# Before the first product of x in a five-mixer network: loads, value products, norm blocks and squares reordered

## The chip, the cores and the metric

The program runs on one core of a Trainium2 chip. Its engines are PE (matrix products), ACT (one-input functions), DVE and POOL (two-input arithmetic), and SP, which here only issues transfers between HBM and the on-chip memory. The metric is the device time of one execution in microseconds (us). What is changed lies wholly in the first part of the program, up to the point where the first product of `x` starts, apart from one rule for norms that holds in later places too.

## The reference, cut to what matters

The reference runs an attention block of two layers on `x` (1024 tokens of width 1024) with a memory `mem` (256 rows of width 1024), and then a pooling mixer and a convolutional feed-forward block. This is what the change touches:

```
memn = rmsnorm(mem, mem_norm_gain)                     # 256 x 1024
for l in range(2):
    h = rmsnorm(x, norm_gain[l])                       # 1024 x 1024
    mk, mv = split(memn @ w_mem_kv[l], 2, axis=-1)     # 256 x 512 each, 4 heads of 128
    qa, ka, ... , qm, gate = split_cols(h @ w_in[l], ...)
    ...
    ym = softmax(qm @ mk.T * 128 ** -0.5) @ mv         # for each of the 4 heads
    ...
# rmsnorm(x, g) = x * rsqrt(mean(x * x) + 1e-6) * g
```

All of it is float32. The kernel keeps that precision by writing each operand as a high part and a low part in the matmul's own format and adding three products (high by high, high by low, low by high).

## The kernel before, in words

**Layout.** `x` and `mem` lie transposed: 128 of the 1024 features to a partition block `c` (eight blocks), tokens along the free dimension. `x` is handled as two halves of 512 tokens; `mem` is one piece of 256 rows. The weights come as units of 256 KB (128 partitions by 512 numbers) from HBM into a ring of three slots, tile `WR`. Each unit is cut into two sub-units of 256 columns. For each sub-unit ACT writes the high part into `WS` (a ring of six), and POOL or DVE subtracts it from the original to give the low part (L2235 on POOL, L1895 on DVE). PE then multiplies (L1420 to L1422, three products for each block of features).

**Order.** A list `steps` is filled once by ordinary Python, and each engine's program walks it from front to back, doing its own share of each step and waiting on semaphores. So the order on every engine, and in SP's queue of transfers, is the order in which `put(...)` was called. `pump()` advances the weight products by one sub-unit (and lets deferred work go on by a step); `ahead(i)` puts the split of a sub-unit five before its product, and the load of a unit `NRAW` = 3 before its use. The norms are generators that `yield` between their parts, and the loop `for _ in first_norm()` calls `pump()` once for each `yield`, which is how norm work and products of the memory are interleaved.

**The start.** SP issues `mem`, four small constants, the eight blocks of `x` (tile `X`), and then the weights. The norm of `mem` comes first: eight squares on ACT, added up on DVE (L2060), a sum over partitions on PE (L1586), the root on POOL (L2224), a broadcast on PE (L1600), and then the eight blocks in `norm_split`: scale on DVE (L2096), high part on ACT, low part on DVE or POOL by turns (L2103, L2256). Only then come the first weight splits. ACT starts by waiting for the four constants.

**The memory's products.** 16 projections, for each layer four heads of keys (`mk`) and four heads of values (`mv`), use 32 units, that is 64 sub-units of six 128x256 products. All have the weights as the stationary operand and the memory as the moving one, so the result lies features by rows. For the values that is the wrong way round: ACT copies the result to `F1`, PE turns it in two 128x128 transposes (L1468), and ACT and DVE take the high and low part from there.

**The norm of x**, during these products: 16 squares (block 0 of both halves, block 1 of both halves, ...), then root, broadcast and eight blocks of the first half, then the same for the second half. After 40 `yield`s it is done, the products of the memory that are left follow, and then the first product of `x` (`HT` by `WS`) starts.

Of the kernel before, what the change touches and what calls it, by code (L numbers as in the profile page):

```python
# [15 lines left out]
MEM = 256  # L16
# [10 lines left out]
NRAW, NSPL = 3, 6  # L27
B_S, B_PT, B_O, B_X = 2, 4, 6, 7
# [130 lines left out]
def build(nc, d):  # L159
    ctx = ExitStack()  # L160
    with ctx:
# [33 lines left out]

        GQ = EO[:, 3072:3200].rearrange("p (a f) -> p a f", a=2)
# [69 lines left out]
        d_const, d_mem = signal("d_const"), signal("d_mem")  # L266
        d_x = [signal(f"d_x{c}") for c in range(8)]
        d_raw = [signal(f"d_raw{i}") for i in range(NRAW)]
# [38 lines left out]

        def ahead(i):
            while at["split"] < min(i + NSPL - 1, len(subs)):
                no = at["split"]  # L310
                u = subs[no][0]
                while at["load"] <= min(u + NRAW - 1, len(units) - 1):
                    v = at["load"]
                    put("load", v)
                    raw_at.append(d_raw[v % NRAW].add(16 * len(units[v](v % NRAW))))
                    at["load"] += 1
                s_whi.add()
                on = s_wlov if no < at["both"] and no % 3 else s_wlop
                half_lo.append((on, on.add()))
                put("split", no)  # L320
                at["split"] += 1

        def w_cols(src, k0, kn, cols):
            n = sum(c[1] for c in cols)

            def pieces(slot):
                v = WR[:, slot, 0:kn * n].rearrange("p (k n) -> p k n", n=n)
# [8 lines left out]
        def w_rows(src, tiles, c0):  # L336
            kn, width = len(tiles), src.shape[1]

            def pieces(slot):
                o, out = 0, []  # L340
                for i, (row, m) in enumerate(tiles[0]):
                    step = tiles[1][i][0] - row
                    out.append((WR[o:o + m, slot, 0:128 * kn].rearrange("p (k n) -> p k n", n=128),
# [19 lines left out]
        OPS = {"hl": (1, 1), "q": (2, 2), "k": (4, 4), "kg": (4, 4), "qg": (2, 2), "v": (1, 0), "vg": (3, 0), "rope": (1, 0), "gate": (1, 1), "x": (0, 1)}  # L363
# [8 lines left out]
        def leave(h):  # L372
# [24 lines left out]
            if h.kind in ("hl", "q", "qg"):  # L397
                ready[h.to[0]] = [(s_ed, s_ed.n)]
# [684 lines left out]
        d_mem.add(16)  # L1083
        for c in range(8):
            square(mem_norm, c, (d_mem, 16))
        for _ in close(mem_norm):
            pass
        for _ in norm_split(mem_norm, C_MEMG, mem_at, MRING, [], [(d_mem, 16)] * 8):
            pass
        for layer in (0, 1):  # L1090
# [14 lines left out]
        def first_norm():  # L1105
            yield
            yield
            for c in range(8):
                for n in (0, 1):
                    square(x_norm[n], c, xt[c])  # L1110
                    yield
            for n in (0, 1):
                yield from close(x_norm[n])
                yield
                yield from norm_split(x_norm[n], C_G0, ht_half(n), HRING, [(s_nd, 8)] if n == 0 else x_norm[0].lo[4:], xt)
# [218 lines left out]
        at["both"] = len(subs)  # L1334
# [4 lines left out]
        for _ in first_norm():  # L1339
            if at["task"] < mem_tasks:  # L1340
                pump()
# [58 lines left out]

        def v_parts(h, i):
# [5 lines left out]
            if h.width == 256:  # L1407
                v = v_at(slot).rearrange("p (h t x c) -> p h t x c", h=4, t=2, x=2)[:, h.to[3]]
# [1046 lines left out]
```

## Time and profile before

| | before |
|---|---|
| median of 3 runs | 2588.92 us (2580.43 to 2593.25) |
| the profiled execution | 2589.86 us, its span 2588.1 us |
| mean granted PE clock | 0.979 of full |
| PE busy (share of the span) | 2424.2 us (94%) |
| DVE busy | 1328.4 us (51%) |
| ACT busy | 1214.3 us (47%) |
| POOL busy | 854.7 us (33%) |
| transfers | 191.93 MB, mean 74 GB/s |

The span is what the trace covers of the profiled execution, and 1.8 us lie around it. Over the whole span PE is nearly always busy; its busy share in the first of 40 slices (64.7 us each) is five tenths and in the second eight tenths, while nearly all others are eight or nine tenths. Times of instructions overlap in the pipelines (the start of the next one, not the end of the last, gives the pace).

### The profile page before, as it was taken

How to read it: one execution, taken by the hardware profiler on the slowest of the kernel's cores; microseconds unless marked ns; L12 is line 12 of the kernel's file. 1: busy time of each engine (PE TensorE's matmuls, PEld its weight loads, DVE VectorE, ACT ScalarE, POOL GpSimd, SP SyncE). 2: the span in 40 equal slices, each digit the busy share in tenths (PEclk: the TensorE clock that was granted, in tenths of full speed). 3: DMA queues.
4: the chain of work that ended last, by engine and by line, in shares of the span. 5: the costliest groups of instructions: out<-in, count | busy, mean ns of one | idle time of the engine just before them, and what ended most of it. 6: DMA issues, size and time to landing. Idle time of an engine off the chain costs nothing.

```text
span 2588.1 us, 36197 instructions
## 1 busy us (share of the span) xinstructions
PE 2424.2 (94%) x12584; PEld 2038.8 (79%) x12584; DVE 1328.4 (51%) x2748; ACT 1214.3 (47%) x2884; POOL 854.7 (33%) x1053
## 2 busy tenths in 40 slices
PE   5898889999999999999999999998889999999999
PEld 5787777777887878888888888776667888888877
DVE  5443576776787524345555555677775313312331
ACT  4443455665676434445556556554454313322321
POOL 2332211111125553221222222556675422322322
PEclk8898999999999999999999999999999999999999
DMA  4421210111124242222222223522223211111112
GB/s 155 131 70 46 57 29 17 33 33 35 44 66 147 78 127 90 89 71 78 86 86 79 78 86 104 165 74 73 66 81 91 74 49 45 49 46 52 49 49 86
DMA packets 309924, 191.93 MB, mean 74 GB/s; under 512 B 63728, under 2 KB 288240, under 8 KB 309232
## 3 DMA queue, kind: packets, MB, share of 16 engines
q1 hardware_dynamic: 309744, 189.61, 25.0%
q8 instruction: 103, 1.69, 0.3%
q14 instruction: 77, 0.63, 0.1%
HBM read 170.16 MB, written 19.40 MB: 73 GB/s over the span
## 4 chain that ended last, share of the span: by engine, by line
PE 75%; DVE 9%; ACT 5%; issue 5%; POOL 3%; DMA 2%; SPq 0%; DVEq 0%; ACTq 0%; POOLq 0%
PE PS L1420 20%; PE PS L1422 19%; PE PS L1421 19%; PE PS L1559 4%; PE PS L1526 4%; PE PS L1513 2%; POOL WS L2235 2%; PE PS L1514 2%; PE PS L1570 2%; ACT PY L1648 1%; DVE ST L1986 1%; ACT PT L1648 1%; DVE PY L2060 1%; ACT WS L1648 1%; ACT EO L1648 1%
## 5 line engine op out<-in xcount | busy, mean ns | idle before, releaser
L2235 POOL TENSOR_TENSOR WS<-WR,WS 128x256 fp32r<-128x256 f32 (+1 forms) x946 | 731.7, 792 | 1609.7 <-ACT WS L1648 1608.6
L1420 PE MATMUL PS<-HT,WS 128*128 128x512 f32 x2080 | 838.3, 403 | 44.2 <-POOL WS L2235 22.4
L1422 PE MATMUL PS<-HT,WS 128*128 128x512 f32 x2080 | 816.0, 392 | 0.0
L1421 PE MATMUL PS<-HT,WS 128*128 128x512 f32 x2080 | 815.2, 392 | 0.0
L1648 ACT ACTIVATE WS<-WR 128x256 fp32r<-128x256 f32 x988 | 368.3, 408 | 384.5 <-PE PS L1422 343.6
L1420 PEld LDWEIGHTS PS<-HT,WS 128*128 128x128 f32 x2080 | 394.0, 189 | 143.4 <-issue 34.4
L1422 PEld LDWEIGHTS PS<-HT,WS 128*128 128x128 f32 x2080 | 393.2, 189 | 84.8
L1421 PEld LDWEIGHTS PS<-HT,WS 128*128 128x128 f32 x2080 | 394.4, 190 | 74.3
L1648 ACT ACTIVATE PT<-PS 128x512 fp32r<-128x512 f32 x352 | 186.3, 530 | 244.0 <-PE PS L1526 243.6
L1864 DVE TENSOR_TENSOR PT<-PS,PT 128x512 fp32r<-128x512 f32 x352 | 208.4, 608 | 93.8 <-ACT PT L1648 92.6
L1420 PE MATMUL PS<-QKV,WS 128*128 128x512 f32 (+1 forms) x608 | 232.7, 383 | 21.8 <-POOL WS L2235 11.2
L1421 PE MATMUL PS<-QKV,WS 128*128 128x512 f32 (+1 forms) x608 | 228.9, 376 | 0.0
L1422 PE MATMUL PS<-QKV,WS 128*128 128x512 f32 (+1 forms) x608 | 228.5, 376 | 0.0
L1559 PE MATMUL PS<-PT,QKV 128*128 128x256 f32 (+1 forms) x1248 | 211.4, 291 | 12.2 <-DVE YB L2050 11.3
L1559 PEld LDWEIGHTS PS<-PT,QKV 128*128 128x128 f32 x1248 | 180.6, 193 | 24.6 <-issue 18.1
L1648 ACT ACTIVATE QKV<-PS 64x512 fp32r<-64x512 f32 (+2 forms) x212 | 122.3, 577 | 157.2 <-PE PS L1422 128.1
L1526 PE MATMUL PS<-ID,PY 128*128 128x128 f32 x1072 | 186.5, 278 | 0.0
L1420 PEld LDWEIGHTS PS<-QKV,WS 128*128 128x128 f32 x608 | 120.3, 198 | 45.7 <-ACT WS L1648 20.7
L1513 PE MATMUL PS<-QKV 128*128 128x384 f32 (+2 forms) x320 | 123.0, 386 | 23.4 <-ACT PY L1648 13.6
L1865 DVE SCALAR_TENSOR_TENSOR QKV<-PS,QKV 64x512 fp32r<-64x512 f32 (+1 forms) x112 | 77.2, 689 | 128.1 <-ACT QKV L1648 125.7
L1648 ACT ACTIVATE PY<-PY,ST 128x384 f32<-128x384 f32 (+1 forms) x192 | 115.5, 601 | 48.2 <-DVE ST L2006 38.2
L1421 PEld LDWEIGHTS PS<-QKV,WS 128*128 128x128 f32 x608 | 120.6, 198 | 18.8
(160 smaller groups left out, 2739.8 us busy)
## 6 DMA issues: line engine op xcount, KB each, us to landing
WR<-in_ffn_in SPq DMA_DIRECT2D x120, 256.0 KB, 2.9
WR<-in_w_in_odd SPq DMA_DIRECT2D x106, 256.0 KB, 3.0
EO<-in_grid SPq DMA_DIRECT2D x48, 384.0 KB, 3.1
WR<-in_w_in_even SPq DMA_DIRECT2D x100, 128.0 KB, 2.6
WR<-in_w_out_odd SPq DMA_DIRECT2D x48, 256.0 KB, 2.9
yd<-PY SPq DMA_DIRECT2D x44, 256.0 KB, 3.4
WR<-in_w_in_even SPq DMA_DIRECT2D x34, 256.0 KB, 3.0
WR<-in_w_mem SPq DMA_DIRECT2D x32, 256.0 KB, 2.9
```

What stands on the lines that cost most here:

```text
L1420: e.matmul(out, wh, rh, start=start, stop=False)
L1421: e.matmul(out, wh, rl, start=False, stop=False)
L1422: return e.matmul(out, wl, rh, start=False, stop=stop)
L1513: e.matmul(out, q, kh, start=True, stop=False)
L1514: m = e.matmul(out, q, kl, start=False, stop=True)
L1526: m = e.transpose(PS[:, B_PT + pb, o + 128 * z:o + 128 * z + 128], p_at(job.c, job.scores[x].slot, p0, p0 + 128), ID[:, :])
L1559: m = e.matmul(out, vv, p, start=a, stop=b)
L1570: m = e.matmul(PS[n * h:n * h + n, B_X, 128 * x:128 * x + 128], RD[:, f.pp % 2, x, h:h + 1].to_broadcast([128, n]), ID[:, :], start=True, ...
L1648: return e.activation(out, in_, func, **more)
L1864: return e.tensor_tensor(out, src, f32(hi), ALU.subtract)
L1865: return e.scalar_tensor_tensor(out=out, in0=src, scalar=scale, in1=f32(hi), op0=ALU.mult, op1=ALU.subtract)
L2235: e.tensor_tensor(WS[:, i % NSPL, 1, 0:n], WR[:, u % NRAW, o:o + n], f32(WS[:, i % NSPL, 0, 0:n]), ALU.subtract).then_inc(s_wlop.sem, 1)
```

## The change

Six things are changed, all in the order of the steps or the place of data:

- The weights of the memory use seven slots (`RAW`: the three of `WR` and four pieces of tiles that are idle then), and six units are loaded ahead of `x`. The later weights keep three slots.
- `mem` is loaded in two halves, ACT no longer waits for the constants at its start (each weight split does), and a one-column square on ACT comes ahead of everything.
- The first five weight splits stand behind the sum of the memory's norm and ahead of its root and blocks.
- The memory's values are produced with the memory as the stationary operand and two heads' weights as the moving one (`mv`, step kind `memT`): 2 projections a layer with 8 sub-units each. The copy to `F1` and the transposes are gone; ACT and DVE take high and low part of 512 columns at once.
- In `norm_split` the scaling of block `c` is put a step ahead of its high part. This holds for every norm that uses it: memory, `x`, the second layer's and the feed-forward's.
- The squares go by halves: eight of the first half, then the first half's root and blocks interleaved with the squares of the second half. There are 42 `yield`s now, with one and two `pump()`s by turns. Low parts of the memory's weights go to POOL and DVE by turns (before: one in three to POOL).

```
+MEM_UNITS, MEM_RAW = 32, 7
+        RAW = [WR[:, i, :] for i in range(NRAW)] + [PY[:, 1024:1536], PY[:, 1536:2048], F1[:, :], SG[:, 0:512]]
+        def raw_slot(u):
+            return u % MEM_RAW if u < MEM_UNITS else (u - MEM_UNITS) % NRAW
         def ahead(i):
             while at["split"] < min(i + NSPL - 1, len(subs)):
                 no = at["split"]
                 u = subs[no][0]
-                while at["load"] <= min(u + NRAW - 1, len(units) - 1):
...
+                while at["load"] <= min(u + (MEM_RAW if at["load"] < MEM_UNITS else NRAW) - 1, len(units) - 1):
+                    load_next()
                 s_whi.add()
-                on = s_wlov if no < at["both"] and no % 3 else s_wlop
+                on = s_wlov if no < at["both"] and no % (2 if no < 2 * MEM_UNITS else 3) else s_wlop
...
         def norm_split(nm, col, dst, ring, before, need):
-            for c in range(8):
-                nm.nd[c], nm.nh[c] = s_nd.add(), s_nh.add()
-                on = s_nlv if c % 2 else s_nlp
-                nm.lo[c] = (on, on.add())
-                put("nsplit", nm, c, need[c])
+            for c in range(9):
+                if c < 8:
+                    nm.nd[c] = s_nd.add()
+                    put("nscale", nm, c, need[c])
                 if c:
-                    put("nsplit lo", nm, c - 1)
-                yield
-            put("nsplit lo", nm, 7)
+                    nm.nh[c - 1] = s_nh.add()
+                    put("nsplit", nm, c - 1)
+                if c > 1:
+                    low_part(nm, c - 2)
+                if c:
+                    yield
+            low_part(nm, 7)
...
-            for h in range(4):
-                c0 = [(512 + 128 * h, 128)]
-                proj(f"mv{layer}{h}", [w_cols(w, 0, 4, c0), w_cols(w, 4, 4, c0)], "v", (f"mv{layer}", None, layer, h), ("mem", 0), MEM)
+            for g in range(2):
+                c0 = [(512 + 256 * g, 256)]
+                proj(f"mv{layer}{g}", [w_cols(w, k, 2, c0) for k in (0, 2, 4, 6)], "mv", (f"mv{layer}", None, layer, g), ("memT", 0), 512)
+        for c in range(8):
+            square(mem_norm, c, (d_mem[c // 4], 16))
+        for _ in range(6):
+            load_next()
+        put("x load")
+        closing = close(mem_norm)
+        next(closing)
+        ahead(0)
...
             for c in range(8):
-                for n in (0, 1):
-                    square(x_norm[n], c, xt[c])
-                    yield
-            for n in (0, 1):
-                yield from close(x_norm[n])
+                square(x_norm[0], c, xt[c])
+                yield
+            split = first_half()
+            for c in range(8):
+                next(split)
+                yield
+                square(x_norm[1], c, xt[c])
+                yield
+            flush_acc()
+            for _ in split:
+                yield
+            yield from close(x_norm[1])
...
-        for _ in first_norm():
-            if at["task"] < mem_tasks:
-                pump()
+        for i, _ in enumerate(first_norm()):
+            for _ in range(1 + i % 2):
+                if at["task"] < mem_tasks:
+                    pump()
...
+                        if h.rhs[0] == "memT":
+                            for x in (0, 1):
+                                m = three(PS[:, h.bank, 256 * x:256 * x + 256], mh[:, 128 * x:128 * x + 128], ml[:, 128 * x:128 * x + 128],
+                                          wh, wl, j == 0 and x == 0, end and x == 1)
...
-            w.wait_ge(d_const, 64)
+            w.wait_ge(s_init, 1)
+            act(YB[:, 0:1], ON[:, :], ACT.Square)
```

SP, the start of its queue, before (`WR` are weight slots, `X` is x):

```order
L2287 DMA EO<-in_memT 128x8x256
L2288 DMA COL<-in_cols 128x240
L2289 DMA ID<-in_ident 128x128
L2290 DMA PCT<-in_pct 128x64
L2291 DMA SK<-in_sink 128x8
L2293 DMA X<-in_xT 128x1024 x8
L2304 DMA WR<-in_w_mem 128x4x128 x32
```

SP at the same place with the change (`PY`, `F` and `SG` hold four more weight slots):

```order
L2349 DMA EO<-in_memT 128x4x256 x2
L2350 DMA COL<-in_cols 128x240
L2351 DMA ID<-in_ident 128x128
L2352 DMA PCT<-in_pct 128x64
L2353 DMA SK<-in_sink 128x8
L2369 DMA WR<-in_w_mem 128x4x128 x3
L2369 DMA PY<-in_w_mem 128x4x128 x2
L2369 DMA F<-in_w_mem 128x4x128
L2357 DMA X<-in_xT 128x1024 x8
L2369 DMA SG<-in_w_mem 128x4x128
```

Six weight units moved ahead of the eight loads of x; the seventh follows them.

ACT, its first instructions, before (`PY<-EO` are the memory's squares, `QKV<-EO` its high parts, `WS` the weights' high parts, `PY<-X` squares of x):

```order
L1648 ACT_TABLE_LOAD
L1648 ACTIVATE PY<-EO 128x256 x8
L1648 ACTIVATE QKV<-EO 128x256 x8
L1648 ACTIVATE WS<-WR 128x256 x6
L1648 ACTIVATE PY<-X 128x512
L1648 ACTIVATE WS<-WR 128x256
```

ACT at the same place with the change:

```order
L1699 ACT_TABLE_LOAD
L1699 ACTIVATE YB<-ON 128x1
L1699 ACTIVATE PY<-EO 128x256 x8
L1699 ACTIVATE WS<-WR 128x256 x5
L1699 ACTIVATE QKV<-EO 128x256 x8
L1699 ACTIVATE WS<-WR 128x256
L1699 ACTIVATE WS<-PY 128x256
L1699 ACTIVATE PY<-X 128x512
```

Five weight splits moved from behind the memory's high parts to ahead of them.

DVE, the start of the first half's blocks of x, before (`SS` the mean, `EO<-X` a scaled block, `HT` a low part of x, `WS` a low part of weights, `QKV<-PS` a result):

```order
L2067 TENSOR_SCALAR SS<-PS 128x4
L1895 TENSOR_TENSOR WS<-WR,WS 128x256 x2
L1864 TENSOR_TENSOR QKV<-PS,QKV 128x2x128
L2096 SCALAR_TENSOR_TENSOR EO<-X,COL,PS 128x512
L1895 TENSOR_TENSOR WS<-WR,WS 128x256
L2096 SCALAR_TENSOR_TENSOR EO<-X,COL,PS 128x512
L1895 TENSOR_TENSOR WS<-WR,WS 128x256
L2096 SCALAR_TENSOR_TENSOR EO<-X,COL,PS 128x512
L2103 TENSOR_TENSOR HT<-EO,HT 128x512
```

DVE at the start of these blocks with the change (`PY<-PY` adds up squares, now those of the second half):

```order
L1951 TENSOR_TENSOR WS<-WR,WS 128x256
L2156 SCALAR_TENSOR_TENSOR EO<-X,COL,PS 128x512 x2
L2120 TENSOR_TENSOR PY<-PY 128x512
L1951 TENSOR_TENSOR WS<-PY,WS 128x256
L1920 TENSOR_TENSOR QKV<-PS,QKV 128x4x128
L2156 SCALAR_TENSOR_TENSOR EO<-X,COL,PS 128x512
L1951 TENSOR_TENSOR WS<-PY,WS 128x256
L2120 TENSOR_TENSOR PY<-PY 128x512
L1951 TENSOR_TENSOR WS<-F,WS 128x256
```

Two blocks are scaled before the first one is split, and additions of the second half's squares stand between. From the first product of x on, PE's instructions are the same in the same order; in DVE's four later norm halves one scaling each stands earlier.

## Rows read from the trace of the kernel before

**Rows 1.** The page's head.

```profile
span 2588.1 us, 36197 instructions
```

**Rows 2.** Waits of PE between 22 and 113.7 us: total, times, longest.

```profile
PE PS L1586 <- DVE PY L2060: 3.4, 1, 3.4
PE PS L1586 <- DVE QKV L1864: 2.3, 1, 2.3
```

**Rows 3.** Stretches: length, busy (count) by engine, PEclk, DMA share, GB/s.

```profile
22.00:42.40 20.40, 16.07 (x108) 15.03 (x108) 16.94 (x32) 15.98 (x41) 6.22 (x7) 1.00 0.44 129
42.40:50.00 7.60, 7.57 (x38) 7.57 (x39) 1.42 (x4) 0.92 (x3) 1.86 (x2) 0.55 0.24 71
50.00:68.60 18.60, 9.00 (x52) 8.37 (x51) 13.29 (x21) 9.45 (x23) 6.85 (x6) 0.77 0.20 56
93.00:113.70 20.70, 19.03 (x138) 18.38 (x138) 9.31 (x21) 10.76 (x32) 7.75 (x12) 0.89 0.54 154
```

**Rows 4.** The timeline at the start: start us, length us, engine, line, operation.

```profile
6.28 1.28 ACT L1648 ACT_TABLE_LOAD   x1 [6.28 <-DMA EO<-in_memT]
8.33 3.61 DVE L2060 TENSOR_TENSOR PY<-PY 128x256 f32<-128x256 f32 x7 [7.43 <-ACT PY L1648]
13.37 0.71 POOL L2224 TENSOR_TENSOR SM<-SM,MH 128x2 f32<-128x2 f32 x1 [12.93 <-DVE SM L2067]
15.39 1.26 DVE L2096 SCALAR_TENSOR_TENSOR EO<-EO,COL,PS 128x256 f32<-128x256 f32 x3 [2.17 <-PE PS L1600]
22.06 0.55 PE L1420 MATMUL PS<-QKV,WS 128*128 128x256 f32 x1 [6.71 <-POOL WS L2235]
```

**Rows 5.** Stretches at the start, columns as in rows 3.

```profile
0.00:6.00 6.00, 0.00 (x0) 0.00 (x0) 0.09 (x2) 0.00 (x0) 0.20 (x4) 1.00 0.69 208
6.00:12.00 6.00, 0.00 (x0) 0.00 (x0) 2.98 (x7) 4.17 (x9) 0.00 (x0) 1.00 0.98 349
```

**Rows 6.** The timeline of PE: a pair each at two paces.

```profile
26.05 0.28 PE L1421 MATMUL PS<-QKV,WS 128*128 128x256 f32 x1
26.17 0.28 PE L1422 MATMUL PS<-QKV,WS 128*128 128x256 f32 x1
...
44.36 0.41 PE L1422 MATMUL PS<-QKV,WS 128*128 128x256 f32 x1
44.58 0.41 PE L1420 MATMUL PS<-QKV,WS 128*128 128x256 f32 x1
```

**Rows 7.** The timeline of DVE and POOL where both work.

```profile
85.81 1.27 POOL L2256 TENSOR_TENSOR HT<-EO,HT 128x512 fp32r<-128x512 f32 x1 [1.32 <-ACT HT L1648]
...
86.07 1.28 DVE L1895 TENSOR_TENSOR WS<-WR,WS 128x256 fp32r<-128x256 f32 x1 [0.40 <-ACT WS L1648]
...
107.49 0.74 POOL L2235 TENSOR_TENSOR WS<-WR,WS 128x256 fp32r<-128x256 f32 x1 [2.92 <-ACT WS L1648]
...
107.72 0.42 DVE L1864 TENSOR_TENSOR QKV<-PS,QKV 128x256 fp32r<-128x256 f32 x1 [2.53 <-ACT QKV L1648]
```

**Rows 8.** The timeline of DVE, back to back.

```profile
30.19 0.41 DVE L1895 TENSOR_TENSOR WS<-WR,WS 128x256 fp32r<-128x256 f32 x1
30.53 0.68 DVE L2060 TENSOR_TENSOR PY<-PY 128x512 f32<-128x512 f32 x1
31.13 0.41 DVE L1895 TENSOR_TENSOR WS<-WR,WS 128x256 fp32r<-128x256 f32 x1
```

**Rows 9.** The first product of x, and the stretch behind it.

```profile
113.44 0.48 PE L1420 MATMUL PS<-HT,WS 128*128 128x512 f32 x1
...
113.40:200.00 86.60, 86.60 (x451) 74.28 (x451) 29.51 (x70) 33.88 (x94) 32.45 (x43) 1.00 0.33 102
```

**Rows 10.** Groups of PE between 22 and 113.7 us: count, busy, mean ns.

```profile
L1586 PE MATMUL PS<-ON,PY 128*128 128x1 f32 x16 | 3.3, 330 | 5.7 <-DVE PY L2060 3.4 <-DVE QKV L1864 2.3
L1600 PE MATMUL PS<-ID,SS 128*128 128x128 f32 x16 | 3.2, 370 | 0.0
```

**Rows 11.** Waits of PE between 960 and 985 us.

```profile
PE PS L1420 <- POOL HT L2256: 2.5, 2, 1.5
```

More of the change, by code:

```diff
@@ L264, in bias_at @@
             return EO[:, o:o + 768].rearrange("p (h n) -> p h n", h=2)
-        d_const, d_mem = signal("d_const"), signal("d_mem")
+        d_const, d_mem = signal("d_const"), [signal(f"d_mem{i}") for i in range(2)]
         d_x = [signal(f"d_x{c}") for c in range(8)]
-        d_raw = [signal(f"d_raw{i}") for i in range(NRAW)]
+        d_raw = [signal(f"d_raw{i}") for i in range(MEM_RAW)]
         d_y = [signal(f"d_y{i}") for i in range(2)]
@@ L306, in add_units, with load_next @@
             return first, tiles
+        def raw_slot(u):
+            return u % MEM_RAW if u < MEM_UNITS else (u - MEM_UNITS) % NRAW
+        def load_next():
+            v = at["load"]
+            put("load", v)
+            raw_at.append(d_raw[raw_slot(v)].add(16 * len(units[v](raw_slot(v)))))
+            at["load"] += 1
         def ahead(i):
@@ L1082, in build @@
         mem_norm = Norm(lambda c: MX[:, c, :], MEM, SM, 0, B_O)
[L1083 to L1089, printed above, removed]
         for layer in (0, 1):
@@ L1094, in build @@
                 proj(f"mk{layer}{h}", [w_cols(w, 0, 4, c0), w_cols(w, 4, 4, c0)], "hl", (f"mk{layer}", None, layer, 1.0, h), ("mem", 0), MEM)
-            for h in range(4):
-                c0 = [(512 + 128 * h, 128)]
-                proj(f"mv{layer}{h}", [w_cols(w, 0, 4, c0), w_cols(w, 4, 4, c0)], "v", (f"mv{layer}", None, layer, h), ("mem", 0), MEM)
+            for g in range(2):
+                c0 = [(512 + 256 * g, 256)]
+                proj(f"mv{layer}{g}", [w_cols(w, k, 2, c0) for k in (0, 2, 4, 6)], "mv", (f"mv{layer}", None, layer, g), ("memT", 0), 512)
+        assert len(units) == MEM_UNITS
+        at["both"] = len(subs)
+        for i in range(2):
+            d_mem[i].add(16)
+        for c in range(8):
[6 more added lines that the diff above has]
+        ahead(0)
+        for _ in closing:
+            pass
+        for _ in norm_split(mem_norm, C_MEMG, mem_at, MRING, [], [(d_mem[1], 16)] * 8):
+            pass
         x_norm = [Norm(half_of(n), 512, SS, 512 * n, B_S + n) for n in (0, 1)]
@@ L1694, in scalar_program @@
                     slot = h.to[2]
-                    if h.kind == "hl" and h.rhs[0] == "mem":
+                    if h.kind == "mv":
+                        src, hi, _ = mem_v_parts(h)
+                        act(hi, src).then_inc(s_ea.sem, 1)
+                    elif h.kind == "hl" and h.rhs[0] == "mem":
                         m0 = 256 * h.to[4]
@@ L2286, in sync_program @@
             w = Waits(e)
-            e.dma_start(MX, d["memT"].rearrange("(c p) n -> p c n", p=128)).then_inc(d_mem.sem, 16)
+            slot_unit = {}
+            for i in range(2):
+                e.dma_start(MX[:, 4 * i:4 * i + 4, :], d["memT"][512 * i:512 * i + 512, :].rearrange("(c p) n -> p c n", p=128)).then_inc(d_mem[i].sem, 16)
             e.dma_start(COL[:, :], d["cols"]).then_inc(d_const.sem, 16)
@@ L2291, in sync_program @@
             e.dma_start(SK[:, :], bass.AP(d["sink"].tensor, 0, [[0, 128], [1, 8]])).then_inc(d_const.sem, 16)
[L2292 to L2293 removed]
             for kind, *of in steps:
[L2295 removed]
+                if kind == "x load":
+                    for c in range(8):
+                        e.dma_start(X[:, c, :], d["xT"][128 * c:128 * c + 128, :]).then_inc(d_x[c].sem, 16)
+                elif kind == "load":
                     u, = of
[L2297 to L2301 removed]
+                    slot = raw_slot(u)
+                    if slot in slot_unit:
+                        v = slot_unit[slot]
+                        w.wait_ge(s_whi, unit_last[v] + 1)
+                        for sig, value in raw_done[v]:
                             w.wait_ge(sig, value)
+                    slot_unit[slot] = u
                     for dst, src in units[u](slot):
```

63 lines of the change are left out of this document (34 added, 29 removed).

## The prediction

> **What bounds the kernel now.** I read the page first for the span [rows 1], then cut the time up to the first product of x into stretches [rows 3], then the timeline by engine. The reader should see a start in two parts. Until 22.06 us PE has no weight product at all [rows 4]. From there to 113.44 us, where the first product of x starts [rows 9], PE has 64 sub-units of six products and little else. At the fast pace two products start 0.12 us apart (26.05, 26.17), so a sub-unit is 0.72 us and all of them 46.1 us; the part takes 91.4 us. It is lost in two ways. PE waits, since the norm of x takes DVE and ACT: 9.00 us of 18.60 busy between 50.0 and 68.6 [rows 3]. And behind idle stretches the granted clock falls from 1.00 (2.4 GHz) to its lower level (1.2 GHz): 0.55, 0.77 and 0.89 on the mean in three stretches [rows 3], where two products start 0.22 us apart (44.36, 44.58) [rows 6]. Behind 113.4 us PE is busy for 86.60 of 86.60 us at clock 1.00 [rows 9]. PE's instructions from there on are the same before and after, and no step there stands at a fixed time, so what the start gains, the end gains: the forecast is the move of that 113.44 us.
>
> **The start, step by step.** Table load: it runs from 6.28 to 7.56 us, behind the landing of `mem` [rows 4]; now a one-column square brings it forward under the transfer: -1.3 us. Halves of `mem`: the DVE's seven additions take 3.61 us and end at 11.94, a pace of 0.53 us [rows 4]. With the first half there early (an estimate: at 4.5 us of the 6.2 that the whole takes) only four additions stand behind the second landing: 6.2, a square of about 0.4, and 4 x 0.53 make 8.9, 3.0 us sooner with the table load in it. If the halves land together only the 1.3 is left. The sum, root and broadcast stay: DVE's first scaling is 3.45 us behind the last addition (15.39 against 11.94), now at 12.4. POOL's root ends 2.14 us behind it (14.08), now at 11.1.
>
> Next the weights: five high parts go ahead on ACT, three low parts on POOL and two on DVE. POOL's low part is 0.74 us [rows 7], so three take POOL to 13.3, one more for the memory's first block to 14.1. The first product is at 14.2 instead of 22.06. The last weights that this needs (units 0 to 2, 0.79 MB, behind 1.05 MB of `mem` and 0.23 MB of constants) are 2.07 MB; 208 GB/s for 6 us bring 1.25 MB, the rest comes at 349 GB/s [rows 5]: 8.3 us. On ACT the eight high parts of the memory are queued behind these splits, and DVE, POOL and PE wait for them; there are 4 us of cover till 12.4. Without the cover each us late is a us lost. Bounds for the first product: 13.4 (low parts ahead of the root) and 17.5 (halves together, and weights late by 1 to 2 us).
>
> x now has six units ahead of it: its first block is complete at 3.37 MB, 12.1 us, and all of it 3.67 MB later at about 349 GB/s, near 22.6 us [rows 5]. Its squares start behind the seventh split, some 18 us, and need a block each 1.6 us or so. ACT would stand with all weight splits behind it if x were late; I cost it at nothing, hidden by the memory's first key products.
>
> **The middle.** What limits 64 sub-units and the norm of x together? One row decides it. A low part on DVE is 0.41 us long (30.19) [rows 8], but the one at 86.07 takes 1.28 and ends at 87.35, 0.27 behind the end (87.08) of POOL's 1.27 us low part of x [rows 7]. DVE instructions with two on-chip-memory inputs and POOL's take turns. The one at 107.72, which has one input in PSUM, keeps its 0.42 under POOL's 0.74 [rows 7]. So there is a shared lane, and its load behind 14.2 us is, with durations where undisturbed and starts back to back [rows 7, 8]:
>
> POOL: 29 low parts of the memory's weights and 4 of the first of x's, 33 x 0.74 = 24.4; 8 low parts of x, 8 x 1.27 = 10.2; 4 of the memory, 3.0. Sum 37.6.
> DVE: 30 low parts at 0.34 (30.19 to 30.53) = 10.2; 14 additions at 0.60 (30.53 to 31.13) = 8.4; 8 low parts of x at the same 0.60 = 4.8; 4 of the memory at 0.34 = 1.4. Sum 24.8.
>
> Together 62.4 us. The scalings (one input in PSUM) and the results stay off the lane. POOL's larger share costs: 11 low parts moved from 0.34 to 0.74 are 4.4 us of it. PE needs 46.1 plus 6.5 for sums and broadcasts [rows 10], ACT less than either; both fit under 62.4 if they interleave. Two times the lane will run dry, at the sums of the two halves, where PE stood 3.4 and 2.3 us [rows 2]; I keep both, 5.7 us. That the lane can be kept full I take from 22.0 to 42.4 us: DVE is 16.94 of 20.40 us busy there [rows 3], at a time when the weights still wait for transfers.
>
> Sum: 14.2 + 62.4 + 5.7 = 82.3 us for the first product of x. That is 31.1 us sooner: 2589.86 - 31.1 = **2558.8 us**, 2559. The profiled execution is 0.9 us above the median of 2588.92, which I leave.
>
> By the Trainium skill's GPSIMD Engine Reference (Key points) GpSimd shares its SBUF interfaces with VectorE, with contention where VectorE has two SBUF inputs; rows 7 agree for this pair. By a rule without sharing, the middle would be PE's: the rival below.
>
> Two edits cost nothing of their own. The turned values need the same products (2 x 8 x 2 x 3 of 256 columns a layer, 96, as before 4 x 8 x 3); they take 16 transposes and 8 copies away, from PE and ACT, which aren't the bound. Seven weight slots take away ACT's waits for transfers, which stand behind 93 us (PE 19.03 of 20.70 busy there [rows 3]); at the end the ring is three again, so one wait of 2 us or less may stay.
>
> Behind the first product: `norm_split` scales a block sooner in four later halves. In one of them PE waits 2.5 us for POOL's low parts [rows 11], whose order stays; a scaling of 0.7 us can come in front of a low part. Between -2.5 and +2.8 us; I take 0.
>
> **Rivals.** *PE alone is the bound.* If the lane overlaps better than rows 7 say, the middle is 46.1 + 6.5, with 1.6 for 16 first products at 0.22 instead of 0.12 [rows 6]: 14.2 + 54.2 = 68.4, time 2544.8. For it: in 22.0 to 42.4 clock 1.00 and PE at 16.07. Against: rows 7.
>
> *The clock's four low stretches come back.* They hold about 34 us of lower clock, 17 us of work; of it 10 us would show, since PE has 10 us of slack against the lane: 2569. For it: gaps near the sums stay. Against: with three `pump()`s for two norm steps PE has work in most of them. In full, at the lower clock throughout, 64 x 6 x 0.22 = 84.5 plus 6.5 from 14.2 is 105.2, 8.2 us sooner: 2582, no difference that can be told. The Trainium skill's TensorE: Matmul & The Clock Gate (Part 1) calls the throttled state the default, which activity releases and idling brings back; rows 3 agree, with 1.00 in the busy stretch and 0.55 behind a gap.
>
> *Slower.* The products of x run at the lower clock. Before they start behind a memory part at 0.89 that ends at 1.00; if the new hand-over, with the last low parts of x and the last values crowded together, leaves PE sparse, the 86.6 us of [rows 9] can start at half speed. Each us of it costs one more; from 31 us on all is lost, all 86.6 would give 2645. Against: a PE that always has work at the lower clock was back at the upper in rows 3 and 6, each time.
>
> *It doesn't do what it says.* x is late and ACT stands: it would have to be 31 us late, at 349 GB/s that is 11 MB. Hardly.
>
> **How the numbers follow.** Forecast 0.62; PE bound 0.14; low stretches back 0.15; clock low throughout 0.05; x late 0.02; slower 0.02. A measurement tells about 0.5% from no change, 12.9 us. Faster by more: the first three, 0.91. Within: 0.07. Slower: 0.02. The range for 8 in 10 reaches from the PE bound to below the case at the low clock: 2544 to 2577. It holds the unknown start (-0.8 to +3.3), the later norms (-2.5 to +2.8) and the runs' own spread of 12.8 us.
>
> **What would show it.** The first weight product near 14 us; ACT's table load before `mem` lands; the first product of x near 82; DVE's low parts of 1 us and more beside POOL's; few waits for transfers on ACT before the end; clock 1.00 over most of 26 to 82. Wrong would be: the first product of x where it was; a granted clock under 0.8 on the mean before it; or a move of it that the span doesn't show.

## The result: 1.4% faster, and where it shows

The changed kernel takes 2551.61 us (2547.12 to 2552.20, 4 runs) against 2585.03 us (2580.43 to 2593.25, 4 runs) on the same chip: a ratio of 0.986, 95% interval 0.9843 to 0.9877. The forecast was 2559, with a range of 2544 to 2577. It was reckoned from the profiled execution of before, 2589.86 us, which lies 4.8 us above the median here; that is two thirds of the 7.1 us between forecast and measurement, and the other 2.3 us are the gain itself, 33.4 us against 31.1. The profiled execution took 2547.12 us with a span of 2545.3, which is 42.8 us less than before's span [rows 1]. It was the fastest of its four, so part of that difference is chance.

The profile page of the changed kernel, its head and first two tables (busy us, share of the span and instructions; then busy tenths in 40 slices):

```profile
span 2545.3 us, 36154 instructions
PE 2409.3 (95%) x12568; PEld 2029.2 (80%) x12568; DVE 1325.8 (52%) x2734; ACT 1209.5 (48%) x2873; POOL 864.6 (34%) x1063
PE   7999888999999999999999999998899999999999
PEclk9999999999999999999999999999999999999999
```

The work is nearly the same, and the second slice of PE is full now; in the first, nine tenths of clock instead of eight.

The start of the changed kernel's timeline, the answers to [rows 4] and to the first of [rows 9] (start us, length us, engine, line, operation, and the idle time before with what ended it):

```profile
0.73 1.28 ACT L1699 ACT_TABLE_LOAD   x1 [0.73 <-PEq L2507]
4.75 1.33 ACT L1699 ACTIVATE PY<-EO 128x256 f32<-128x256 f32 x4 [2.52 <-DMA EO<-in_memT]
5.50 3.61 DVE L2120 TENSOR_TENSOR PY<-PY 128x256 f32<-128x256 f32 x7 [4.60 <-ACT PY L1699]
8.26 2.12 ACT L1699 ACTIVATE WS<-WR 128x256 fp32r<-128x256 f32 x5 [0.29 <-DMA WR<-in_w_mem]
10.54 0.76 POOL L2284 TENSOR_TENSOR SM<-SM,MH 128x2 f32<-128x2 f32 x1 [10.10 <-DVE SM L2127]
11.28 2.08 POOL L2295 TENSOR_TENSOR WS<-WR,WS 128x256 fp32r<-128x256 f32 x3
12.62 1.66 DVE L2156 SCALAR_TENSOR_TENSOR EO<-EO,COL,PS 128x256 f32<-128x256 f32 x4 [1.54 <-PE PS L1651]
14.50 0.55 PE L1464 MATMUL PS<-QKV,WS 128*128 128x256 f32 x1 [1.92 <-POOL QKV L2316]
...
79.19 0.47 PE L1464 MATMUL PS<-HT,WS 128*128 128x512 f32 x1 [0.42 <-ACT WS L1699]
```

The table load lies under the transfer, the first half of `mem` is there at 4.75, the additions end at 9.11 instead of 11.94, the weights are split before the root is there, and the first weight product starts at 14.50 (before: 22.06). The first product of x starts at 79.19 (before: 113.44). So the start gave 7.56 us and the middle 26.7 of the 34.25.

How far ahead of before each product of PE is (the lead), told by pairing the products of the two traces from the end backwards (they are the same from the first product of x on): 34 us at 208 us of before's time, 36.3 at 885, 36.8 at 912, 34.0 at 980, 35.5 at 1400, 38.4 at 1905, 42.6 at 1935, and nearly that to the end. The step of 4.2 us between 1905 and 1935 is no chance, as the runs below show. Two of the smaller ones are the granted clock's. Behind 912 the changed kernel has 6.8 us at the lower level which before has not, and near 1203 before has 3.4 us which the changed kernel has not. The first of these places, before and changed (columns as in [rows 3]):

```profile
955.00:975.00 20.00, 16.79 (x82) 13.58 (x80) 11.36 (x16) 8.67 (x20) 11.27 (x13) 1.00 0.49 161
918.00:938.00 20.00, 17.82 (x73) 14.61 (x72) 8.57 (x13) 7.12 (x16) 8.65 (x10) 0.83 0.47 155
```

The stretches of the changed kernel in the middle (length; busy and count of PE, weight load, DVE, ACT, POOL; PEclk, DMA share, GB/s), the answer to [rows 3]:

```profile
14.00:25.00 11.00, 10.50 (x65) 10.53 (x66) 8.21 (x18) 8.40 (x22) 6.14 (x8) 1.00 1.05 383
25.00:35.00 10.00, 9.37 (x78) 9.11 (x77) 9.51 (x16) 8.22 (x22) 6.12 (x8) 1.00 0.76 224
35.00:45.00 10.00, 10.00 (x86) 10.00 (x86) 7.58 (x12) 6.77 (x17) 4.87 (x7) 1.00 0.54 159
45.00:55.00 10.00, 7.43 (x57) 6.81 (x56) 10.00 (x15) 6.36 (x17) 5.84 (x7) 1.00 0.33 107
55.00:65.00 10.00, 6.15 (x49) 5.60 (x48) 8.29 (x14) 5.16 (x15) 7.27 (x8) 1.00 0.33 106
65.00:79.20 14.20, 12.71 (x93) 12.36 (x91) 13.14 (x18) 9.26 (x22) 9.53 (x11) 0.88 0.19 57
```

PE is busy 29.87 of 31.00 us up to 45. Then the first half's blocks meet the squares of the second half, DVE is busy 10.00 of 10.00, then 8.29 of 10.00, and PE goes down to 7.43 and 6.15. The granted clock has one low stretch (3.4 us, from 65 us) where before had four with 34 us together. Here too it stands behind a stretch in which PE was often idle (6.15 of 10.00 busy). PE was busy 3.40 of the 3.40 us, so it lost at most 1.7 us.

One more slow piece isn't in the clock column. The first 28 weight products, from 14.50 to 20.61, start 0.21 us apart and then 0.12, while the granted clock reads 1.00 all along:

```profile
20.18 0.41 PE L1466 MATMUL PS<-QKV,WS 128*128 128x256 f32 x1
20.40 0.37 PE L1464 MATMUL PS<-QKV,WS 128*128 128x256 f32 x1
20.61 0.28 PE L1465 MATMUL PS<-QKV,WS 128*128 128x256 f32 x1
20.73 0.28 PE L1466 MATMUL PS<-QKV,WS 128*128 128x256 f32 x1
```

Before did the same with its first 17, from 22.06 to 25.82. At 0.12 us each the 28 would take 2.7 us less; the prediction prices all products at 0.12.

PE's three longest waits from 14 to 79.2 us (total, times, longest):

```profile
PE PS L1464 <- DVE WS L1951: 4.7, 5, 1.7
PE PS L1651 <- POOL SS L2284: 2.3, 1, 2.3
PE PS L1464 <- POOL QKV L2316: 1.9, 1, 1.9
```

The first is for low parts of weights on DVE, whose instructions are stretched beside POOL's, as the next lines show. The second is for the root of x's norm, once; the third is at the very start. The two stops at the sums in [rows 2], 3.4 and 2.3 us, are both gone, and the one of 2.3 us at the broadcast is new.

The groups of DVE and POOL from 13.5 to 79.2 us in the changed kernel (count, busy us, mean ns, idle before):

```profile
L2120 DVE TENSOR_TENSOR PY<-PY 128x512 f32<-128x512 f32 x14 | 13.1, 938 | 0.2
L2163 DVE TENSOR_TENSOR HT<-EO,HT 128x512 fp32r<-128x512 f32 x8 | 8.1, 1009 | 0.1
L2156 DVE SCALAR_TENSOR_TENSOR EO<-X,COL,PS 128x512 f32<-128x512 f32 x16 | 11.5, 736 | 1.5 <-PE PS L1651 1.5
L2316 POOL TENSOR_TENSOR HT<-EO,HT 128x512 fp32r<-128x512 f32 x8 | 11.7, 1460 | 0.7 <-ACT HT L1699 0.7
```

An addition that takes 0.68 undisturbed [rows 8] takes 0.94 on the mean, a low part of x 1.01, POOL's 1.46 instead of 1.27 [rows 7]; the scaling, with one input in PSUM, keeps its 0.736. That is the shared lane at work.

How much of the middle does the lane fill? If the intervals of all its instructions (POOL's, and DVE's with two inputs in on-chip memory) are laid over one another, they cover 54.6 of the 64.7 us between 14.50 and 79.19, so the lane is empty for 10.1 us. In before they cover 55.5 of 91.4. The work on the lane is nearly the same, and the gain of the middle is the time in which nothing ran there. Up to 45 us the lane is in use 25.0 of 30.5 us and PE is nearly full. Behind 45 it is in use 29.6 of 34.2, and DVE with its scalings and results 31.4. So PE bounds the first part and a stretched DVE the second, not the lane the whole.

### The profile page after: what moved, and what is told of

Read it like the earlier page. It is cut to its first block, busy times and chain, and to the rows that moved or that the text cites. A ratio compares the mean times of both kernels' runs of the same rounds, so it can differ in the third digit from the quotient of the medians.

```text
span 2545.3 us, 36154 instructions
## 1 busy us (share of the span) xinstructions
PE 2409.3 (95%) x12568; PEld 2029.2 (80%) x12568; DVE 1325.8 (52%) x2734; ACT 1209.5 (48%) x2873; POOL 864.6 (34%) x1063
## 4 chain that ended last, share of the span: by engine, by line
PE 79%; DVE 9%; issue 5%; ACT 4%; POOL 3%; DMA 1%; SPq 0%; DVEq 0%; POOLq 0%; ACTq 0%
PE PS L1464 21%; PE PS L1466 20%; PE PS L1465 20%; PE PS L1610 5%; PE PS L1577 4%; PE PS L1564 2%; PE PS L1565 2%; PE PS L1621 2%; POOL WS L2295 1%; ACT PY L1699 1%; DVE ST L2046 1%; ACT PT L1699 1%; DVE PY L2120 1%; ACT EO L1699 1%; DVE QKV L1920 1%
## 5 line engine op out<-in xcount | busy, mean ns | idle before, releaser
L1699 ACT ACTIVATE WS<-WR 128x256 fp32r<-128x256 f32 (+1 forms) x954 | 355.3, 408 | 375.4 <-PE PS L1466 342.8
L1464 PE MATMUL PS<-QKV,WS 128*128 128x512 f32 (+1 forms) x544 | 209.1, 384 | 13.7 <-DVE QKV L2276 4.6
L1465 PE MATMUL PS<-QKV,WS 128*128 128x512 f32 (+1 forms) x544 | 207.2, 381 | 0.0
L1466 PE MATMUL PS<-QKV,WS 128*128 128x512 f32 (+1 forms) x544 | 207.0, 381 | 0.0
L1564 PE MATMUL PS<-QKV 128*128 128x384 f32 (+2 forms) x320 | 122.4, 384 | 23.3 <-ACT PY L1699 13.6
L2262 DVE TENSOR_TENSOR X<-X,PS 128x1024 f32<-128x1024 f32 x24 | 29.3, 1221 | 204.7 <-PE PS L1466 204.7
L1464 PEld LDWEIGHTS PS<-QKV,WS 128*128 128x128 f32 x544 | 104.4, 192 | 36.2 <-ACT WS L1699 9.3
```

The lines of the kernel that those rows point to most:

```text
L1464: e.matmul(out, wh, rh, start=start, stop=False)
L1465: e.matmul(out, wh, rl, start=False, stop=False)
L1466: return e.matmul(out, wl, rh, start=False, stop=stop)
L1564: e.matmul(out, q, kh, start=True, stop=False)
L1699: return e.activation(out, in_, func, **more)
```

## The experiments

Each run's first number is the start of the first product of x in its trace; the changed kernel's is 79.19 and before's 113.44. Whole executions of one kernel differ by up to 14 us. How exact the first number is, one pair tells: the fifth experiment's kernel is the same as the changed one up to there and has 78.97, 0.2 us away. No kernel was traced in two executions. A low stretch of the clock takes up to half its length where PE has work, 1.7 us of 3.4, and such stretches fall differently from kernel to kernel, so differences under 2 us are weak. Each experiment undoes one part of the change, or moves low parts between the engines. Six kernels ran once: old order with one and two steps 2551.55 us, no scaling ahead anywhere 2557.91, values the old way 2556.63, old start 2557.39, three slots 2561.48, x loaded first 2558.90.

**One in three low parts on POOL.**

```
-                on = s_wlov if no < at["both"] and no % (2 if no < 2 * MEM_UNITS else 3) else s_wlop
+                on = s_wlov if no < at["both"] and no % 3 else s_wlop
```

> The changed kernel, but only one in three low parts of the memory's weights goes to POOL (21 of 64 instead of 32); DVE does the rest. Theory (lane): DVE's two-input work on on-chip memory and POOL's work take turns, and that lane sets the middle part. 11 low parts of 0.74 become 0.34 us, the lane's load falls by 4.4 us, so the first product of x comes at 79.2 - 4.4 = 74.8 us (73 to 77). Rival (DVE by itself is the bound and POOL only stands beside it): DVE gets 11 x 0.34 = 3.7 us more work, first product at about 83 us (81 to 85). Rival (PE bound): no move, 79 +- 1.

Measured: first product of x at 76.15, 3.0 us sooner, with no low stretch of the clock; 2548.00 us (2543.99 to 2548.72, 4 runs), ratio to before 0.985 (0.9835 to 0.9864). It went the way of the lane and not the way of DVE by itself, which had more work and was done sooner. The expected 4.4 us was too much: `no % 3` leaves 22 of 64 parts on POOL, so ten moved and not 11, nine of them behind the first product, which is 3.6 us of the lane's load. Of the 3.0 us up to 1.7 can be the low stretch of the clock that the changed kernel has and this one has not. What speaks for the lane beyond that is that the mean addition fell from 938 to 726 ns and PE's waits for DVE's low parts from 4.7 to 1.3 us:

```profile
PE PS L1464 <- DVE WS L1951: 1.3, 2, 0.9
L2120 DVE TENSOR_TENSOR PY<-PY 128x512 f32<-128x512 f32 x14 | 10.2, 726 | 0.0
```

**All low parts on DVE.**

```
+                on = s_wlov if no < at["both"] else s_wlop
```

> The changed kernel with all 64 low parts of the memory's weights on DVE; POOL keeps the low parts of the norms. Lane theory: 32 parts of 0.74 become 0.34, load of the lane 62.4 - 0.40 x 29 = 50.8 us, but then PE's 52.6 and DVE's own undisturbed work (24.8 + 29 x 0.34 = 34.7 on the lane, 11.5 of scalings, 5.4 of results, 51.6 us, and 13 us of POOL's turns on top, 64.6 at worst) are next: first product of x at 14.2 + 54 to 65, 68 to 78 us. Rival (DVE by itself the bound): 29 x 0.34 = 9.9 us later, 89 us. The start moves too: five low parts ahead of the memory's blocks are all DVE's, 1 us either way.

Measured: 77.90, with a low stretch of the clock at 74.5; 2549.33 us (2542.93 to 2549.92, 4 runs), ratio 0.9852 (0.9836 to 0.9869). It is within the range of the lane theory, and far from 89. But 11.6 us less load on the lane gave only 1.3. The next bound is probably DVE, busy 60.17 of 66.00 us, with PE (58.92) close to it:

```profile
14.00:80.00 66.00, 58.92 (x425) 55.80 (x426) 60.17 (x120) 45.06 (x114) 19.02 (x18) 0.97 0.52 166
```

**Squares in the old order, one step of products for one of the norm.**

```
+            for c in range(8):
+                for n in (0, 1):
+                    square(x_norm[n], c, xt[c])
+                    yield
+            for n in (0, 1):
+                yield from close(x_norm[n])
+                yield
+                yield from norm_split(x_norm[n], C_G0, ht_half(n), HRING, [(s_nd, 8)] if n == 0 else x_norm[0].lo[4:], xt)
...
-            for _ in range(1 + i % 2):
+            for _ in range(1):
```

> The changed kernel with the squares of x in the old order (both halves of each block, then one half's root and blocks after the other) and one step of weight products for each step of the norm; all else stays new. Theory (interleaving): the two norm chains again stand alone beside PE, as before, so most of the gain in the middle goes: the middle was 91.4 us before and is 64.7 now; I expect 20 of these 26.7 us back, first product of x at 99 us (92 to 105), with lower clock in stretches again. Rival (the early start, the seven slots and the turned values bring the most): 85 us or less.

Measured: 91.33, that is 12.1 us back, less than the 20 I expected; 2561.65 us (2561.33 to 2563.60, 4 runs), ratio 0.9908 (0.9891 to 0.9924). It is the largest single part and still not most of the 26.7. The low stretches of the clock are back (17 us together), and with them PE's waits for a root and for a sum of x's norm:

```profile
PE PS L1636 <- POOL SS L2269: 3.4, 1, 3.4
PE PS L1622 <- DVE PY L2105: 2.9, 1, 2.9
```

**The old order of squares with one and two steps by turns** (the same edit without its last two lines).

> As the kernel with the old order of squares, but with one and two steps of weight products by turns, as in the changed kernel. This parts the order of the squares from the number of products put beside them. If the number is what counts: first product of x within 3 us of the changed kernel's 79.2. If the order by halves is what counts: over 88 us. I expect the first, with 81 us: the lane's load is the same in either order.

Measured: 84.35. Between the two: undone in this order, 7.0 of the 12.1 us come from the number of products beside the norm and 5.2 from the order by halves. The clock has a share in the 7.0: this kernel has one low stretch of 3.4 us, the one above 17 us of them, and half of the 13.6 us between them is 6.8. My 81 was too low; the order matters although the lane's load is the same, so the load alone doesn't give the time.

**No scaling ahead in the four later norm halves.** In `norm_split`:

```
+            if col in (C_G1, C_FFNG):
+                for c in range(8):
+                    nm.nd[c] = s_nd.add()
+                    put("nscale", nm, c, need[c])
+                    nm.nh[c] = s_nh.add()
+                    put("nsplit", nm, c)
+                    if c:
+                        low_part(nm, c - 1)
+                    yield
+                low_part(nm, 7)
+                return
```

> The changed kernel, but in the four later norm halves (second layer, feed-forward) each block is scaled in the step of its high part again, as before. The changed kernel gained 34.2 us up to the first product of x, but 42.7 us to the end of the profiled span. Theory (the later norms gave 4 to 6 us of the rest, above all the feed-forward's second half): the first product of x stays at 79.2 and the lead falls by 2 to 5 us behind the feed-forward's norms. Rival (the rest is where the clock's lower stretches happen to fall): the lead behind them is that of the changed kernel within 1 us.

Measured: first product of x at 78.97, and a lead that is 33.1 us at 1905 and 33.1 at 1935 of before's time. In all nine other variants that keep the scaling ahead, and in the changed kernel, the lead grows there by 4.2 to 4.3 us (4.23 to 4.29). The waits of PE in this place, and of ACT for scalings, of this kernel (1871 to 1902 us) and of the changed one (1866.5 to 1894 us); before's PE has the same three waits, 2.2, 1.4 and 0.8 us, between 1905 and 1935:

```profile
PE PS L1475 <- ACT WS L1710: 2.2, 1, 2.2
PE PS L1475 <- POOL WS L2306: 1.4, 2, 0.8
PE PS L1648 <- DVE PY L2131: 0.9, 1, 0.9
ACT HT L1710 <- DVE EO L2167: 8.7, 6, 2.3
```

```profile
PE PS L1637 <- DVE PY L2120: 0.8, 1, 0.8
ACT HT L1699 <- DVE EO L2156: 4.6, 4, 1.6
```

The place is the feed-forward's second half: ACT stood at a high part for its scaling, with weight splits queued behind it, and PE wanted these. The other three later halves show less. At 885 to 912 us all ten traces with the scaling ahead gain 0.4 to 0.5 us. Around 950 to 1000 they lose 2 to 5 us and this kernel 3.2, and the loss goes with the granted clock: before has no low stretch there; the traces with 6.8 us of it lose 2.4 to 3.2, those with 10.2 us 3.6 to 3.7, those with 13.6 us 5.1 to 5.3. At 1200 to 1400 the ten gain about 1.6 us, and this kernel nothing: before and this kernel have a low stretch of 3.4 us near 1203, the ten have none. Why the clock falls in one and not in the other isn't shown. The whole time, 2551.71 us (2549.26 to 2558.07, 4 runs), can't show 4 us in this spread.

**No scaling ahead anywhere** (the same with `if True`).

> The changed kernel with the old scaling in step in every norm, the memory's and x's too. Theory: a high part then waits for its own scaling at ACT's front, 0.7 us and the handing over each, as before (18.0 us of such waits on 13 blocks), and the splits behind it wait as well: the memory's blocks take 1.5 us more and x's 16 blocks some 0.3 us each where the lane is the bound, first product of x at 85 us (82 to 88). Rival (the lane hides it): 80 us or less.

Measured: 84.84. ACT waits 19.7 us for scalings of x in 15 places, where the changed kernel waits 13.5 in 8:

```profile
ACT HT L1710 <- DVE EO L2167: 19.7, 15, 2.0
```

5.65 us later than the changed kernel, as expected; about 6 us more of low clock are in it. At 1905 to 1935 the lead shrinks by 0.95 us, with a low stretch of 3.4 us there, and from 885 to 1400 it keeps still: it has before's clock there, none low around 950 to 1000 and 3.4 us near 1203.

**The memory's values the old way.**

```
-            for g in range(2):
-                c0 = [(512 + 256 * g, 256)]
-                proj(f"mv{layer}{g}", ... "mv", ..., ("memT", 0), 512)
+            for h in range(4):
+                c0 = [(512 + 128 * h, 128)]
+                proj(f"mv{layer}{h}", ... "v", ..., ("mem", 0), MEM)
```

> The changed kernel with the memory's values produced the old way: 8 projections of 4 sub-units, copy, two transposes each, then high and low part (one weight slot lies in the upper half of SG instead of F1, which the copy needs). Theory: it costs ACT 8 copies and PE 16 transposes off the bound, and 8 low parts of 256 instead of 4 of 512 columns: first product of x within 2 us of 79.2, at 80.5. Rival (the transposes' waits at PE, 8.9 us before, and one F1 for all, stall the chain): 84 to 90.

Measured: 84.12, the rival's number. PE waits at the transposes 3.4 us for the copy on ACT, and DVE waits for high parts 9.3 us:

```profile
PE PS L1522 <- ACT F L1702: 3.4, 4, 1.3
DVE QKV L1923 <- ACT QKV L1702: 9.3, 6, 3.4
```

**The old start.**

```
-        closing = close(mem_norm)
-        next(closing)
-        ahead(0)
-        for _ in closing:
+        for _ in close(mem_norm):
             pass
...
-            w.wait_ge(s_init, 1)
-            act(YB[:, 0:1], ON[:, :], ACT.Square)
+            w.wait_ge(d_const, 64)
```

(and all eight squares of `mem` wait for its second half)

> The changed kernel with the old start: ACT waits for the constants, no early square, both halves of mem awaited, weight splits behind the memory's blocks. The rest stays new. Theory: the first weight product goes from 14.5 back to 21 us (it was 22.06; blocks scaled ahead save 1), and since the lane's load of five low parts then also lies behind it, the first product of x comes 6.5 to 8 us later, at 86.5. Rival (the middle hides part of it): 83 or less.

Measured: first weight product at 21.35, first product of x at 84.21. 6.85 us late at the start are 5.0 at the end of the middle: it hides 1.8 us. Why isn't shown: that x and the weights lie ready by then isn't enough, for in the next run they do too, and there the middle hides 0.1 us.

**x loaded first.** The six `load_next()` ahead of `put("x load")` are gone.

> The changed kernel with the loads of x ahead of all weights, as before; seven slots stay. Theory: x's 4.2 MB take about 11 us at 350 to 415 GB/s, so the first weights land at 18 to 20 us instead of 8; ACT stands at the first weight split with the memory's eight high parts behind it, and the first weight product comes at 23 to 26 us instead of 14.5. The squares of x can't use that time, they stand behind it. First product of x 9 to 11 us later, at 89 us. Rival (the middle catches up, since weights and x are then all there): 83 or less.

Measured: ACT's first weight split at 19.06, the first weight product at 23.22, the first product of x at 87.78, 8.6 us late. The split came 10.8 us later than in the changed kernel and the first weight product 8.7, so 2.1 us were hidden. ACT stood with the memory's high parts behind it:

```profile
19.06 1.56 ACT L1697 ACTIVATE WS<-WR 128x256 fp32r<-128x256 f32 x4 [10.99 <-DMA WR<-in_w_mem]
```

**Three slots for the memory's weights** (`MEM_RAW = 3`, three loads ahead of x).

> The changed kernel with three slots for the memory's weights instead of seven (three units are loaded ahead of x, the fourth behind it). Theory: transfers hardly limit where DVE and POOL's lane does, but behind x's 4 MB the fourth unit, which the changed kernel had before x, arrives near 20 us and is wanted at 17: a stall of 3 to 5 us at the start, and up to 3 us in the middle: first product of x at 84 us (81 to 88). Rival (slots are free, 256 KB in 3 us always in time): 79 to 80. Rival (transfers bound the products as they did behind 93 us, where 24 sub-units took 20.7 us, 0.86 each): 64 x 0.86 = 55, hidden under 64.7, same 79.

Measured: 85.89, 6.7 us late. The edit changes two things, the number of slots and the units ahead of x (three instead of six), and they weren't parted. ACT waits for weights in 11 places, the longest, 4.4 us until 21.93, for the fourth unit, which now is issued behind x:

```profile
ACT WS L1699 <- DMA WR<-in_w_mem: 14.1, 11, 4.4
```

**One in three on POOL, and fewer low parts of x there.**

```
+        def lo_pool(nm, c):
+            return c % (4 if nm.col == C_G0 else 2) == 0
```

> The changed kernel with one in three low parts of the memory's weights on POOL (first product of x at 76.2 us so far) and, besides, two of eight low parts of each half of x on POOL instead of four. Lane theory: four parts go from POOL's 1.27 to DVE's 0.60 us, the lane's load falls by 2.7 us, first product of x at 73.5 us (72 to 76). Rival (now DVE is full by itself): four times 0.60 more on DVE, 78 to 79. Rival (PE by now): 76. The time would be 2.5 us under the one-in-three kernel's, 2545 against 2548, which the runs' spread may hide.

Measured: 75.71; 2547.49 us (2543.26 to 2550.39, 5 runs), ratio 0.9844 (0.9821 to 0.9868). 0.4 us less than the one-in-three kernel, where the lane says 2.7. The number is that of the rival with PE as the bound, but in these stretches DVE is the full engine, so which of the two it is stays open; a low stretch of 3.4 us, which the one-in-three kernel hasn't, can hide up to 1.7 us. Stretches of this kernel:

```profile
45.00:55.00 10.00, 7.10 (x51) 6.07 (x49) 10.00 (x17) 6.03 (x16) 4.22 (x5) 1.00 0.37 117
65.00:75.20 10.20, 8.83 (x71) 8.31 (x70) 10.20 (x18) 7.07 (x18) 5.31 (x6) 1.00 0.28 78
```

DVE is full in both, POOL half idle. This version has the lowest median of all, and it and the one-in-three version start x's products 3.5 and 3.0 us sooner than the changed kernel. By whole times the three can't be told apart, since their intervals overlap.

## Why the prediction was right, and where it was not

*The start* was read right: 14.2 forecast, 14.50 measured, by the steps named (table load, halves, splits ahead of the blocks). The additions ended at 9.11 (8.9 forecast), the root at 11.30 (11.1), x's loads hid. The cover named for the weights was real but smaller than the 4 us: with x loaded first, weight splits 10.8 us later made the start 8.7 us later.

*The bound of the middle* was read right in kind and only in part in size. That POOL's and DVE's instructions on on-chip memory stretch each other is shown by the lengths above, and taking work off POOL shortened the middle although DVE got more to do. The forecast had the lane in use for 62.4 us and dry for 5.7, 68.1 together; the trace has it in use for 54.6 and empty for 10.1, 64.7 together. That 62.4 lies near the measured 64.7 is partly luck, because two errors of opposite sign meet, -7.8 and +4.4 us:

- The load was priced too high. Between 14.50 and 79.19 POOL starts 32 parts of 256 columns and not the 37 of the sum, since two of the memory's come before and three of x's first four weight parts behind; DVE starts 33 and not 34. At the same prices the load is 58.3 us. And the two don't strictly take turns: 58.3 us of load and the roots (2.2 us) fit into 54.6 us, so some 5 us ran side by side.
- The empty time was priced too low. "That the lane can be kept full" was read from DVE's 16.94 of 20.40 us between 22.0 and 42.4 [rows 3], but DVE's busy time also holds what isn't on the lane. Laid over one another, the lane's instructions cover 16.8 of 20.3 us there, 82%; in the changed kernel's middle they cover 84%.

The lane's load alone doesn't give the time either: with the old order of squares and one and two steps by turns the load is the same and the middle took 69.8 us. With 11.6 us less of it the middle took 63.4, since DVE's own work and PE stand close behind. The lane is one of three near bounds, and PE is the one up to 45 us.

*The two dry times*, 5.7 us, were put in the wrong place: PE didn't wait for the sums at all, as the squares of the second half fill the gaps, but 2.3 us for POOL's root once and 4.7 us for low parts on DVE. Lane and dry times together were 3.4 us too long, and the start 0.3 too short: that is the 3.1 us between 82.3 and 79.2. "11 low parts moved" to POOL should have been ten, which didn't touch the sum.

*"Two edits cost nothing of their own"* was wrong, though it didn't touch the sum, since it was made for the new kernel and not from edit to edit. Undone, the turned values cost 4.9 us, and three slots with three units ahead of x 6.7. I priced the transposes by PE's time, and not by the wait for the copy in front of them. The trace of before had it, from 22 to 113.7 us:

```profile
PE PS L1468 <- ACT F L1648: 8.9, 3, 5.0
```

In the run with the old values 3.4 of the 4.9 us stand as this wait; a low stretch more of the clock can hold up to 1.7.

*The later norms* were the term that failed: taken at 0, with 2.5 us as the best end. One of them gave 4.2 us. I looked at the place where PE waits for low parts [rows 11], and it waits for them still:

```profile
PE PS L1464 <- POOL HT L2316: 2.1, 2, 1.9
```

I did not look at the feed-forward's second half, where PE waited 2.2 us for weight splits on ACT and 1.4 for their low parts on POOL. The scaling ahead shortened ACT's waits there from 8.7 to 4.6 us, which isn't the chain I priced. The forecast's 31.1 us, 3.1 in the middle and 4.2 here make 38.4 of the 42.8 us between the two profiled spans; the rest is what is left of small steps up and down, of which two are the clock's (-2.8 and +1.6 us) and the cause of the others stays open. By medians the gain is 33.4 us, and the interval of the ratio makes it 31.8 to 40.6, so the forecast of 31.1 was slightly low and whole times don't decide more.

*The rivals.* PE alone as the bound would have been 68.4: no, though PE was the bound up to 45 us. The clock's low stretches came back only as one of 3.4 us, and where I undid the interleaving there were two with 17 us. Slower: the first 86.6 us of x's products ran at clock 1.00, as the answer to the second of [rows 9] has it:

```profile
79.10:165.70 86.60, 85.76 (x444) 73.28 (x445) 30.32 (x71) 34.33 (x96) 34.85 (x45) 1.00 0.32 102
```

x was never late: ACT has no wait for it from 14 to 79.2 us.

The parts undone one by one sum to 43 us (halves and steps 12.1, x's place 8.6, slots 6.7, scaling 5.65, start 5.0, values 4.9) against 34.25 for all. They overlap: undoing one part also spoils some of what another gives. Above all, "x's place" and "slots" both cut the units loaded ahead of x, from six to none and to three, so part of them is counted twice. What each would bring alone in the old kernel wasn't tried.

## What to carry to other kernels

Where one engine's two-input work on on-chip memory and another's stretch each other in the trace, add both into one sum and compare that with each engine's own; then move work to the engine that does it in less of the shared time, until the next bound shows. The sum is a load and not yet a time: look in the trace how much of a stretch the shared instructions cover together (here 82 to 84%), and do it by stages, since another engine may be the bound in one of them. When two traces differ by a few us, look first whether a low stretch of the clock lies in one and not in the other. When an instruction waits at the front of an in-order queue, price it by what stands behind it: the scaling a step ahead saved more through the weight splits behind it than through the norm. And judge small edits by an anchor inside the trace (here the first product of x, and the lead of paired products) when whole executions differ by more than the effect.

## What the runs showed that I had not expected

The same 4.2 us step appeared at the same place in ten traces with the scaling ahead, whatever came earlier, to 0.1 us: one execution's trace is enough for such a step, though the total of that execution isn't. And the number of weight products put beside a step of the norm (7.0 us of 12.1, up to 6.8 of it by the clock) counted for more than the order of the squares.
